# Gate matrix of a PEER layer: one-hot rows of four tokens per instruction, high and low products summed by accumulating matmuls

## What is computed

```
s = einsum('thpc,pnc->thpn', q, sub_keys)         # 512 tokens, 8 heads, 2 halves, 128 keys
top_s, top_i = top_k(s, 16)
cand_s = top_s[:, :, 0, :, None] + top_s[:, :, 1, None, :]
best_s, best_pos = top_k(cand_s, 16)              # expert = i * 128 + j
gate = softmax(best_s)
a = einsum('tkd,td->tk', expert_u[idx], xs)
out = einsum('tk,tkd->td', gelu(a) * gate, expert_v[idx])
```

## Time and profile before

| | us |
|---|---|
| median of 3 runs | 4918.12 |
| lowest, highest | 4912.20, 4918.73 |
| span of the profiled execution | 4916.6 |
| TensorE busy in it | 4781.9 |
| the stage of the gate matrix in it | 2427 to 3236 |

### The profile page before, as it was taken

One profiled execution on the slowest core, in us unless ns is written; L12 is line 12 of the kernel. 1 busy time (PEld: TensorE's weight loads), 2 busy tenths in 40 slices (PEclk: granted clock), 3 DMA queues, 4 the chain that ended last, 5 costly groups with the idle time before them and its releaser, 6 DMA issues.

```text
span 4916.6 us, 63731 instructions
## 1 busy us (share of the span) xinstructions
PE 4781.9 (97%) x21848; PEld 3957.1 (80%) x21848; DVE 2320.9 (47%) x4554; ACT 1529.5 (31%) x2064; POOL 2029.6 (41%) x844
## 2 busy tenths in 40 slices
PE   6999999999999999999999999999999999999998
PEld 6877788888878878888888878888788888888886
DVE  6241434433344349900399999930224334333334
ACT  5232333333344232223233333322222222222222
POOL 5323244344434444444433333344444444444443
PEclk9999999999999999999999999999999999999999
DMA  5322233333344432333344444463544444444442
GB/s 186 99 63 84 82 103 102 104 102 101 102 149 162 135 103 86 116 118 124 116 141 150 140 148 139 141 207 119 160 145 147 148 136 147 143 149 145 137 133 86
DMA packets 251757, 626.51 MB, mean 127 GB/s; under 512 B 20128, under 2 KB 86048, under 8 KB 248992
## 3 DMA queue, kind: packets, MB, share of 16 engines
q1 hardware_dynamic: 118656, 432.07, 27.5%
q10 hardware_dynamic: 133024, 193.38, 11.4%
HBM read 533.09 MB, written 92.27 MB: 127 GB/s over the span
## 4 chain that ended last, share of the span: by engine, by line
PE 58%; issue 20%; POOL 9%; DVE 1%; DMA 0%; ACT 0%; POOLq 0%; ACTq 0%; DVEq 0%
PE bank L1543 19%; PE bank L1545 19%; PE bank L1544 19%; POOL w_lo L513 9%; PE bank L1704 1%; DVE arena L1067 0%; DMA arena<-mix_scratch 0%; PE bank L1738 0%; DVE x_lo L1494 0%; DMA arena<-gate_matrix_scratch 0%; POOLq L512 0%; PE bank L1750 0%; DVE arena L1488 0%; POOLq L510 0%; ACT x_hi L580 0%
## 5 line engine op out<-in xcount | busy, mean ns | idle before, releaser
L513 POOL TENSOR_TENSOR w_lo<-w_raw,w_hi 128x1024 fp32r<-128x1024 f32 x824 | 2013.1, 2445 | 2830.8 <-ACT w_hi L537 2830.8
L1543 PE MATMUL bank<-x_hi,w_hi 128*128 128x512 f32 x6464 | 2544.4, 394 | 34.6 <-DVE x_lo L1329 9.8
L1544 PE MATMUL bank<-x_lo,w_hi 128*128 128x512 f32 (+1 forms) x6592 | 2565.3, 389 | 0.0
L1545 PE MATMUL bank<-x_hi,w_lo 128*128 128x512 f32 x6464 | 2526.3, 391 | 0.0
L537 ACT ACTIVATE w_hi<-w_raw 128x1024 fp32r<-128x1024 f32 x824 | 872.0, 1059 | 1956.0 <-PE bank L1545 1869.7
L1543 PEld LDWEIGHTS bank<-x_hi,w_hi 128*128 128x128 f32 x6464 | 1221.7, 189 | 294.5 <-issue 33.0
L1544 PEld LDWEIGHTS bank<-x_lo,w_hi 128*128 128x128 f32 x6592 | 1248.2, 189 | 246.9 <-issue 1.4
L1545 PEld LDWEIGHTS bank<-x_hi,w_lo 128*128 128x128 f32 x6464 | 1220.1, 189 | 257.2
L1515 DVE TENSOR_TENSOR arena<-arena,bank 128x512 f32<-128x512 f32 x256 | 176.0, 688 | 848.3 <-PE bank L1545 848.3
L1473 DVE TENSOR_SCALAR early_mix_or_one_hots<-constants 128x128 fp32r<-128x128 f32 x1024 | 497.0, 526 | 0.0
L1488 DVE TENSOR_TENSOR arena<-arena 128x512 f32<-128x512 f32 x128 | 260.4, 2035 | 25.8 <-DMA arena<-gelu_scratch 18.7
(11 more groups left out here) (215 smaller groups left out, 2069.0 us busy)
## 6 DMA issues: line engine op xcount, KB each, us to landing
w_raw<-w_u SPq DMA_DIRECT2D x256, 512.0 KB, 3.5
w_raw<-w_v SPq DMA_DIRECT2D x256, 512.0 KB, 3.6
w_raw<-w_in SPq DMA_DIRECT2D x200, 512.0 KB, 3.5
gate_matrix_scratch<-arena ACTq DMA_DIRECT2D x16, 2048.0 KB, 7.0
arena<-gate_matrix_scratch ACTq DMA_DIRECT2D x32, 1024.0 KB, 7.7
arena<-gelu_scratch ACTq DMA_DIRECT2D x128, 256.0 KB, 3.7
gelu_scratch<-arena ACTq DMA_DIRECT2D x102, 256.0 KB, 2.1
w_raw<-w_up SPq DMA_DIRECT2D x32, 512.0 KB, 3.5
```

Of the source, the lines that this page charges most:

```text
L513: nc.gpsimd.tensor_tensor(wlo[s][:], raw[s][:], whi[s][:], ALU.subtract).then_inc(w_lo_made, 1)
L1543: M.matmul(out, whi[s][:, k], h, start=f, stop=False)
L1544: M.matmul(out, whi[s][:, k], l, start=False, stop=False)
L1545: ins = M.matmul(out, wlo[s][:, k], h, start=False, stop=e)
```

## The change

Groups, slots, chunks and the loop stay. What is different:

- The turned numbers i and j stay in PSUM (banks 4 and 5) and are read from there; `iit`, `jjt`, `gtt` and the copies into `cur` are gone. Bank 6 holds the gates only until `ghi` and `glo` are made from it.
- One VectorE instruction now makes the rows of four tokens (512 elements) by comparing or multiplying two tensors, one of them broadcast: a comparison for j into PSUM (bank 6 or 7), one for i into `oh_i`, and two multiplications of the found j by the high and by the low gates. The multiplications wait for the first comparison by a new semaphore, `j_found`.
- TensorE computes each token in two matmuls of 128x128 into the same place, the second accumulating. A group now fills one bank (2 or 3) instead of two.
- ScalarE copies the sums out, one instruction a group, and raises `gmat_saved`; VectorE's additions are gone.
- The waits of TensorE and ScalarE are counted anew for this.

```
--- before.py
+++ after.py
@@ -245,7 +245,7 @@
         ghi, glo = early_a[:, 0].bitcast(F32R), early_a[:, 1].bitcast(F32R)
         oh_i = early_b[:, 0:2].rearrange("p a b -> p (a b)").rearrange("p (a b) -> p a b", b=P).bitcast(F32R)
 
-        oh_j = early_b[:, 2:6].rearrange("p a b -> p (a b)").rearrange("p (a h b) -> p a h b", h=2, b=P).bitcast(F32R)
+        oh_j = early_b[:, 2:6].rearrange("p a b -> p (a b)").rearrange("p (h a b) -> p h a b", h=2, b=P).bitcast(F32R)
 
         def early(k):
             return early_a[:, k] if k < 2 else early_b[:, k - 2]
@@ -303,10 +303,9 @@
         gate_soft = sem("gate_soft")
         sel_turned = sem("sel_turned")
         sel_saved = sem("sel_saved")
-        block_cols = sem("block_cols")
         onehots = sem("onehots")
         gmat_done = sem("gmat_done")
-        gmat_hi = sem("gmat_hi")
+        j_found = sem("j_found")
         gmat_saved = sem("gmat_saved")
         gmat_out = [sem(f"gmat_out{b}") for b in range(2)]
         gelu_out = [sem(f"gelu_out{b}") for b in range(2)]
@@ -449,15 +448,11 @@
         plof = tab[:, 576:640].rearrange("p (a b) -> p a b", a=TT)
         bsum = tab[:, 768:800]
         brcp = tab[:, 800:832]
-        cur = tab[:, 896:896 + 4 * TB].rearrange("p (a b) -> p a b", a=4)
         skt = tab[:, 1024:1024 + 2 * NK].rearrange("p (a b) -> p a b", a=2)
 
         eg = qpt
         gstage = carve(2 * T, 2, NK, TB)
-        iit = carve(2 * T + 2 * NK * TB, T)
-        jjt = carve(3 * T + 2 * NK * TB, T)
-        gtt = carve(4 * T + 2 * NK * TB, T)
-        assert 5 * T + 2 * NK * TB <= 2 * T + TT * 2 * PH * NK + 4096
+        assert 2 * T + 2 * NK * TB <= 2 * T + TT * 2 * PH * NK
 
         a = Area()
         y = a(KT, T)
@@ -558,8 +553,9 @@
 
             for s_ in (*gate_out, dil_out, hg_out, *gelu_out, *gmat_out):
                 act.sem_inc(s_, 16)
-            for s_ in (gates_made, gmat_saved, score_saved):
+            for s_ in (gates_made, score_saved):
                 act.sem_inc(s_, 1)
+            act.sem_inc(gmat_saved, 2)
             def square_tile(r, src, k):
                 ring = squares_of(r)
                 n = ring.shape[1]
@@ -894,26 +890,24 @@
             expert_chunks(U_1, U_2)
             expert_chunks(U_1 + U_2, U_3)
 
-            act.wait_ge(sel_saved, 5)
+            act.wait_ge(sel_saved, 2)
             first = U_1 + U_2 + U_3
             with act.Fori(0, NTB // 2) as i:
                 for c in range(8):
                     b = c // 4
 
-                    def save_high(q):
+                    def save_gates(q):
                         if q % 8 == 0:
                             act.wait_ge(gmat_out[b], 16 * i + 16)
-                        act.wait_ge(gmat_done, 16 * i + (q + 1) + 1)
-                        for x in range(2):
-                            pair = bank[2 + 2 * (q % 2) + x][:].rearrange("p (t h j) -> p t h j", t=2, h=2)
-                            t0 = 4 * (q % 8) + 2 * x
-                            last = A.activation(gstage[:, b, :, t0:t0 + 2].rearrange("p j t -> p t j"),
-                                                pair[:, :, 0], ACT.Copy)
-                        last.then_inc(gmat_hi, 1)
-
-                    expert_chunk(first + c, i, 8, lambda: save_high(2 * c), lambda: save_high(2 * c + 1))
+                        act.wait_ge(gmat_done, 16 * i + (q + 1) + 2)
+                        t0 = 4 * (q % 8)
+                        A.activation(gstage[:, b, :, t0:t0 + 4].rearrange("p j t -> p t j"),
+                                     bank[2 + q % 2][:].rearrange("p (t j) -> p t j", j=NK),
+                                     ACT.Copy).then_inc(gmat_saved, 1)
+
+                    expert_chunk(first + c, i, 8, lambda: save_gates(2 * c), lambda: save_gates(2 * c + 1))
                     if c % 4 == 3:
-                        act.wait_ge(gmat_saved, 16 * i + (2 * c + 2) + 1)
+                        act.wait_ge(gmat_saved, 16 * i + (2 * c + 2) + 2)
                         act.dma_start(gmat_dram[2 * i + b], gstage[:, b]).then_inc(gmat_out[b], 16)
 
 
@@ -1001,7 +995,7 @@
         def _(dve):
             V = nc.vector
 
-            for s_ in (dd.sem, hd.sem, tk.sem, onehots):
+            for s_ in (dd.sem, hd.sem, tk.sem):
                 dve.sem_inc(s_, 1)
             dve.sem_inc(out_read, 2)
 
@@ -1437,46 +1431,26 @@
             V.tensor_tensor(e, e, brcp.unsqueeze(2).broadcast_to([P, TT * PH, TOPK]), ALU.mult).then_inc(gate_soft, 1)
 
             dve.wait_ge(sel_turned, 3)
-            V.tensor_copy(iit, bank[4][:]).then_inc(sel_saved, 1)
-            V.tensor_copy(jjt, bank[5][:]).then_inc(sel_saved, 1)
-            V.tensor_copy(gtt, bank[6][:]).then_inc(sel_saved, 1)
-            dve.wait_ge(sel_saved, 3)
-            V.tensor_copy(ghi, gtt).then_inc(sel_saved, 1)
-            dve.wait_ge(sel_saved, 4)
-            V.tensor_tensor(glo, gtt, ghi, ALU.subtract).then_inc(sel_saved, 1)
-            dve.wait_ge(sel_saved, 5)
-
-            def save_products(i, q):
-
-                b = q // 8
-                dve.wait_ge(gmat_hi, 16 * i + (q + 1))
-                for x in range(2):
-                    pair = bank[2 + 2 * (q % 2) + x][:].rearrange("p (t h j) -> p t h j", t=2, h=2)
-                    t0 = 4 * (q % 8) + 2 * x
-                    o = gstage[:, b, :, t0:t0 + 2].rearrange("p j t -> p t j")
-                    last = V.tensor_tensor(o, o, pair[:, :, 1], ALU.add)
-                last.then_inc(gmat_saved, 1)
+            V.tensor_copy(ghi, bank[6][:]).then_inc(sel_saved, 1)
+            dve.wait_ge(sel_saved, 1)
+            V.tensor_tensor(glo, bank[6][:], ghi, ALU.subtract).then_inc(sel_saved, 1)
+            dve.wait_ge(sel_saved, 2)
+
+            def of_four(row, i, q):
+                return row[:, bass.ds((2 * TB) * i + 4 * q, 4)].unsqueeze(2).broadcast_to([P, 4, P])
 
             with dve.Fori(0, NTB // 2) as i:
-                for b in range(2):
-                    for k, s in enumerate((iit, jjt, early_a[:, 0], early_a[:, 1])):
-                        dve.wait_ge(onehots, 16 * i + 8 * b + 1)
-                        V.tensor_copy(cur[:, k], s[:, bass.ds((2 * TB) * i + TB * b, TB)]).then_inc(block_cols, 1)
-                    dve.wait_ge(block_cols, 8 * i + (4 * b + 4))
-                    for g in range(8):
-                        q = 8 * b + g
-                        dve.wait_ge(gmat_done, 16 * i + max(q - 1, 0) + 1)
-                        for x in range(4):
-                            t, slot = 4 * g + x, 4 * (q % 2) + x
-                            V.tensor_scalar(oh_i[:, slot], iota, cur[:, 0, t:t + 1], None, ALU.is_equal)
-                            for h in range(2):
-                                last = V.tensor_scalar(oh_j[:, slot, h], iota, cur[:, 1, t:t + 1],
-                                                       cur[:, 2 + h, t:t + 1], ALU.is_equal, ALU.mult)
-                        last.then_inc(onehots, 1)
-                        if q >= 2:
-                            save_products(i, q - 2)
-                save_products(i, 14)
-                save_products(i, 15)
+                for q in range(16):
+                    slots = slice(4 * (q % 2), 4 * (q % 2) + 4)
+                    at_j = bank[6 + q % 2][:].rearrange("p (a b) -> p a b", b=P)
+                    number = iota.unsqueeze(1).broadcast_to([P, 4, P])
+                    dve.wait_ge(gmat_done, 16 * i + (q + 1))
+                    V.tensor_tensor(at_j, number, of_four(bank[5], i, q), ALU.is_equal).then_inc(j_found, 1)
+                    V.tensor_tensor(oh_i[:, slots], number, of_four(bank[4], i, q), ALU.is_equal)
+                    dve.wait_ge(j_found, 16 * i + (q + 1))
+                    V.tensor_tensor(oh_j[:, 0, slots], at_j, of_four(early_a[:, 0], i, q), ALU.mult)
+                    V.tensor_tensor(oh_j[:, 1, slots], at_j, of_four(early_a[:, 1], i, q), ALU.mult)\
+                        .then_inc(onehots, 1)
 
 
             def product(s, k):
@@ -1575,7 +1549,7 @@
             def tiles_split(r):
                 return lambda k: (odd_low[r] if r in odd_low and k % 2 else norm[r][1]).wait(pe, f"lo{k}")
 
-            pe.sem_inc(gmat_done, 1)
+            pe.sem_inc(gmat_done, 2)
             pe.wait_ge(consts_in, 32)
             column_sum(0, MEM, KT)
             spread(0, MEM)
@@ -1846,14 +1820,14 @@
                     for x in range(2):
                         chunk_half(n, i, 8, x)
                         q = 2 * c + x
-                        pe.wait_ge(onehots, 16 * i + (q + 1) + 1)
-
-                        pe.wait_ge(gmat_saved, 16 * i + max(q, 1))
+                        pe.wait_ge(onehots, 16 * i + (q + 1))
+
+                        pe.wait_ge(gmat_saved, 16 * i + (q + 1))
                         for k in range(4):
-                            o = bank[2 + 2 * (q % 2) + k // 2][:, 2 * P * (k % 2):2 * P * (k % 2) + 2 * P]
+                            o = bank[2 + q % 2][:, P * k:P * k + P]
```

(4 more changed lines are left out.)

## The result

The changed kernel takes 4960.17 us (median; 4954.18 to 4963.67), the kernel before 4915.44 us beside it: a ratio of 1.0087, interval 1.0075 to 1.0099. That is 45 us slower, outside the range of 4870 to 4934 us. The span of its profiled execution is 4961.9 us, 45.3 us more than before.

The account below looks back on a forecast made before the run. The prediction took TensorE, busy 97% of the span, as the bound. Waits won back (-51.7 us) and added weight loads (+57.6 us) gave +5.9 us on a median of 4918.1, so 4924 us, range 4870 to 4934 us.

Parts of the forecast that it names:

- The waits, -51.7 us: Gate-matrix stage: TensorE's seven waits for one-hots between loop iterations, with the slow clock after them, go; 51.7 us won.
- VectorE, four instructions of 0.69 us: VectorE in the gate-matrix stage: four 512-element instructions per group, 2.8 us in all, upper bound 5.2 us.
- Rival 3: Gate-matrix stage: the waits stay because VectorE's new comparisons are far dearer, above 2.5 us each; 4976 us; chance 6%.
- ScalarE, between 0.67 and 1.34 us: ScalarE's save of 512 elements in one instruction takes 0.67 to 1.34 us, nearer the upper end; no effect on time.
- The load as floor, 0.116 us: Eight 128-column products per group: each limited by its weight load to 0.116 us, 0.93 us a group, +57.6 us; 60%.
- The other two bounds, 0.067 us and plain fp32's rate: Eight 128-column products per group: columns alone, 0.54 us a group, or plain fp32 in full, 1.79 us a group.
- rivals 1 and 2: Eight products: first, load no floor, 0.067 us each, 4874 us, 20%; second, plain fp32's rate, 5034 us, 14%.
- The rule of 107 ns per load: Weight loads of the eight products: 107 ns for 128 columns, 0.86 us a group, sum about -4 us.
- 81 ns for a steady stream: The eight products: some 81 ns per pair of load and product, estimated 0.65 us a group and -30 us.
- The sum of the stage, +5.9 us: Gate-matrix stage: -51.7 us from the waits plus 57.6 us from the loads, on a span of 4916.6 us.
- only what lengthens or shortens TensorE's own stream counts: Whole kernel: TensorE busy 97% of the span, its chain three large products and nothing that the change edits.
- the slower rivals: Gate-matrix stage: eight products at plain fp32's rate, 5034 us, 14%; waits staying through dear VectorE comparisons, 4976 us, 6%.

Follow-up runs that it names:

- The rows alone: Kernel before with VectorE writing one-hot rows of four tokens per instruction, products kept at 256 columns with VectorE's additions: 4867.71 us, ratio 0.9897.
- The changed kernel with 16 fillers: Changed kernel with 16 instructions of already fulfilled waits on TensorE right ahead of its last stage: 4919.93 us, ratio 1.0006 to the kernel before.
- 104 fillers: Kernel before with 104 instructions of already fulfilled waits on TensorE ahead of the last stage: 4934.27 us, one run.
- 56: Kernel before with 56 instructions of already fulfilled waits on TensorE ahead of the last stage: 4921.66 us, ratio 1.0006.
- 24 fillers: Kernel before with 24 instructions of already fulfilled waits on TensorE ahead of the last stage: 4920.46 us, a single run.
- 128: Kernel before with 128 instructions of already fulfilled waits on TensorE ahead of the last stage: 4964.7 us, ratio 1.0098.

## Why the prediction was wrong

The forecast was 4924 us, its range ended at 4934; the measured time is 36 us above the forecast. Step by step:

- **The waits, -51.7 us: right.** All seven went, at the boundary too, and the clock stayed at 1.00. The rows alone give 50 us; their stage is 754.4 us long from the first group to the last, 51.8 less than before.
- **VectorE, four instructions of 0.69 us: right.** 0.696, 0.680, 0.683 and 0.679 us; 39.73 of 101 us busy (45 named). None of the four kinds is longer on average than the additions from PSUM by more than 0.01 us, so GpSimd does not hold them. Rival 3 is out.
- **ScalarE, between 0.67 and 1.34 us: right**, 1.129 us, and nobody waits for it.
- **The load as floor, 0.116 us: right**, 0.11 to 0.12; 0.91 us a group against 0.93, and groups 0.45 us further apart than before, as forecast. The other two bounds, 0.067 us and plain fp32's rate, and with them rivals 1 and 2, are out. The rule of 107 ns per load that the prediction took from "TensorE: Matmul & The Clock Gate" in the Trainium skill is near; the same page's 81 ns for a steady stream does not show here.
- **The sum of the stage, +5.9 us: right**, it is 5.7. The changed kernel with 16 fillers, which is the change without the surprise, measures +2.6 us by the medians, within 0.2% as forecast.
- **The step that failed** is the one that stands in the first paragraph, "only what lengthens or shortens TensorE's own stream counts", and the sum that ends with the stage: +5.9 us on a span of 4916.6, all outside taken as unmoved. The term that is missing is where TensorE's later loops lie in their pieces of instructions. It is +40.5 us, seven times the rest of the sum, and none of the rivals named it; the slower rivals had their places in the eight products and in the waits. The reading behind that paragraph was too short: the three large products are 57% of the chain in the earlier trace rows, while the page's line above it gives 20% to "issue" and 9% to GpSimd. Those shares are far more than any stop, so they do not point at one; but they leave a good part of the chain unread. The prediction counted 8 products for 4 in time and not in instructions. The count of 128 could have been read from the order of the changed kernel, and the signs in the trace of before: 53 packets of the instruction queue, and 3.55 us of issue at 375.71 with the slow clock behind it, at the turn of a loop as long as the last one.

What stays open: the end of a piece is inferred from where the stops stand and how the fillers move them. Within 16 fillers on the other side of that end nothing was run, so how abruptly 6.7 us a turn become nothing is bounded only from one side (104 fillers: 1.0 to 1.4 us a turn; 56: at most 0.4). Why the dilated attention's loop is fetched again in some profiled executions and not in others, its place being the same, is open too.

## What to carry to other kernels

A long loop on an engine has a second cost besides its work: its place in the engine's instruction pieces. When an edit changes the number of an engine's instructions ahead of such a loop, compare the packets of the instruction queue and look for idle time named "issue" just behind each turn; a handful of fulfilled waits in the engine's idle time moves the loop, and a slowdown that goes away with them, and that the old kernel shows when it is moved alike, is not the edit's own. And where two edits each remove the same wait, make the one that costs the bounding engine nothing.

## What the runs showed of the hardware

- TensorE's instructions come in packets of 16 KB (1.77 MB in 108). A loop of 1632 instructions ran without any packet at some places (0, 24 fillers) and with nine or ten per iteration at others (56 to 128), at every one of its six turns. The turn of a loop of 1670 instructions, at one and the same place, had a stop in eight profiled executions and none in three.
- After a branch to a piece that is no longer held the next one comes late: TensorE went on 7.5 to 8.5 us after the branch. It had seventeen products of the old iteration left, 3.96 us, and with enough products in the first piece the fetch was hidden altogether (100 and 108 packets with iterations of 174.1 to 174.5 us).
- Idle time of 3.4 to 4.3 us was followed by the 1.2 GHz level at all twelve stops, for some 13 intervals and 2.6 to 3.0 us lost at eleven of them; idle time of 0.5 to 2.03 us by none at eleven stops; at one of 2.05 us the level fell and 1.7 us were lost.
- Instructions of fulfilled waits followed each other 0.106 us apart on TensorE; 176 of them at the start of its work put its first product from 21.0 to 33.4 us, and left it at 21.0 us when they stood ahead of its first real wait.
- Products of float32r with 128 columns, each with its own load, start 0.11 to 0.12 us apart, the first two of a group 0.06; comparisons of 512 elements with a broadcast operand, one input in PSUM, take VectorE as long (0.68 to 0.70 us) as its additions from PSUM.
